# Both ends of a decoder kernel: operand tiles ahead of the squares, three products ahead of the norm's sums, the second weight load behind x, the last weight slot by token block

## The reference, cut to what matters

```python
def rmsnorm(x, g):
    xf = x.astype(jnp.float32)
    y = xf * lax.rsqrt(jnp.mean(xf * xf, axis=-1, keepdims=True) + EPS)
    return (y * g.astype(jnp.float32)).astype(x.dtype)
# first: the input norm and the projections of layer 0
hn = rmsnorm(h, mix_norm[i])
proj = hn @ w_in            # queries, keys, values, gates of two mixers
# last: the expert layer's sum and the final norm
a = (jax.nn.gelu(hid, approximate=False) * g).astype(xb.dtype)
return jnp.einsum('thk,thkd->td', a, ve)
...
return rmsnorm_2(h, final_norm_w)
```

## Time and profile before

| what | value |
| --- | --- |
| median of 3 runs | 3516.91 us (3513.79 to 3517.32) |
| the profiled execution | 3521.62 us |
| its span | 3519.7 us |
| mean granted TensorE clock | 0.993 |

### The profile page before, as it was taken

The page is one execution under the profiler, slowest core; times in us unless marked ns, Lnnn a source line. Parts: engine busy times, 40 slices in busy tenths (PEclk is TensorE's granted clock), DMA queues, the critical chain, the costliest instruction groups (busy, mean ns, idle before and its releaser), DMA issues. The chain is left out here.

```text
span 3519.7 us, 45047 instructions
## 1 busy us (share of the span) xinstructions
PE 3443.8 (98%) x16298; PEld 2801.3 (80%) x16298; DVE 1716.3 (49%) x3318; ACT 925.6 (26%) x1581; POOL 2181.6 (62%) x2180
## 2 busy tenths in 40 slices
PE   7998999999999999999999999999999999999998
PEld 5765888887688888877788777788888888888887
DVE  6563444247754424246324766655555154444443
ACT  3354222124622212135411111133333211111111
POOL 5421766675266667653367777655555588888885
PEclk9999999999999999999999999999999999999999
DMA  6110222222122222221122233344444665555552
GB/s 207 60 37 24 90 96 97 99 92 96 37 102 96 96 96 96 102 72 61 66 84 102 109 137 131 134 165 180 180 180 179 226 217 194 194 195 194 195 198 86
DMA packets 134325, 440.14 MB, mean 125 GB/s; under 512 B 7139, under 2 KB 76932, under 8 KB 97284
## 3 DMA queue, kind: packets, MB, share of 16 engines
q1 hardware_dynamic: 39168, 285.23, 22.9%
q10 hardware_dynamic: 94980, 152.40, 12.2%
HBM read 362.64 MB, written 74.96 MB: 124 GB/s over the span
## 5 line engine op out<-in xcount | busy, mean ns | idle before, releaser
L192 PE MATMUL banks<-memory,weights_split 128*128 128x512 f32 x9456 | 2248.1, 395 | 40.1 <-DMA memory<-in_consts 17.2
L192 PEld LDWEIGHTS banks<-memory,weights_split 128*128 128x128 f32 x9456 | 1760.4, 189 | 435.8 <-issue 51.0
L2984 POOL TENSOR_SCALAR weights_split<-weights_raw 128x512 fp32r<-128x512 f32 x1088 | 740.6, 690 | 1314.9 <-PE banks L192 669.3
L2989 POOL TENSOR_TENSOR weights_split<-weights_raw,weights_split 128x512 fp32r<-128x512 f32 x1088 | 1488.5, 1379 | 0.0
L192 PE MATMUL banks<-weights_split,memory 128*128 128x512 f32 (+1 forms) x3648 | 822.1, 387 | 1.9 <-DVE memory L1365 1.9
L192 PEld LDWEIGHTS banks<-weights_split,memory 128*128 128x128 f32 x3648 | 678.9, 188 | 141.5 <-DVE memory L1365 2.3
L2746 DVE TENSOR_TENSOR memory<-memory,memory 128x512 fp32r<-128x512 f32 x128 | 167.5, 1309 | 355.0 <-ACT memory L2860 355.0
L2725 DVE TENSOR_SCALAR memory<-banks,memory 128x128 f32<-128x128 f32 x512 | 174.3, 402 | 214.0 <-PE banks L2592 204.9
L2860 ACT ACTIVATE memory<-memory 128x512 fp32r<-128x512 f32 x128 | 80.8, 632 | 601.0 <-PE banks L192 587.9
L2793 ACT ACTIVATE memory<-banks 128x512 f32<-128x512 f32 x128 | 76.5, 597 | 569.2 <-PE banks L192 569.2
L2740 DVE TENSOR_TENSOR memory<-memory,memory 128x512 f32<-128x512 f32 x128 | 164.9, 1289 | 51.2 <-DMA memory<-hidden 44.7
(11 more groups left out here) (243 smaller groups left out, 2195.0 us busy)
## 6 DMA issues: line engine op xcount, KB each, us to landing
weights_raw<-in_weights SPq DMA_DIRECT2D x272, 1024.0 KB, 4.8
hidden<-memory ACTq DMA_DIRECT2D x64, 512.0 KB, 2.6
routing<-memory ACTq DMA_DIRECT2D x16, 2048.0 KB, 6.3
memory<-routing ACTq DMA_DIRECT2D x32, 1024.0 KB, 8.0
memory<-hidden ACTq DMA_DIRECT2D x32, 1024.0 KB, 10.2
window_rows<-memory ACTq DMA_DIRECT2D x1, 3064.0 KB, 25.3
chunk_rows<-memory ACTq DMA_DIRECT2D x1, 2556.0 KB, 12.8
residual<-in_x ACTq DMA_DIRECT2D x4, 512.0 KB, 11.2
```

The costliest lines, as they stand in the source:

```text
L192: last = k.nc.tensor.matmul(out, left[a], right[b], start=start and n == 0, stop=stop and n == 2, skip_group_check=True)
L2984: k.nc.gpsimd.tensor_scalar(cut(high, n * PIECE, PIECE), cut(raw, n * PIECE, PIECE), 1.0, 1.0, ALU.mult, ALU.mult).then_inc(k.high_made, 1)
L2989: k.nc.gpsimd.tensor_tensor(cut(low, n * PIECE, PIECE), cut(raw, n * PIECE, PIECE), cut(high, n * PIECE, PIECE).bitcast(F32), ALU.subtract ...
```

## The change

The first norm gets a stage of its own: ScalarE waits for the columns, does a one-element Square, makes the eight high parts, and then the eight squares, each in a buffer of its own; VectorE makes all low parts and then adds the squares. TensorE does three products, then waits for the constants, then does the sums, the bias rows and the other seven products. Its wait for the clearing of the scores and the scans moves into step 1 of the schedule, behind the first share. VectorE's part of the bias rows stands behind the evacuation of product 2. SP waits for the first part of x ahead of its load of slot 1. At the end, ScalarE does a one-element Sqrt after its last operand, and TensorE walks the last slot block by block with both keys in each bank.

```diff
-def first_norm(k, normed, await_input, await_consts):
+def first_norm(k, normed, await_columns, await_input, await_consts):
     normed.begin()
+    with k.scope(at=B_AT):
+        squares, spare = [k.take(512) for _ in range(D_TILES)], k.take(8)
...
     def scalar(act):
+        a = k.nc.scalar
+        await_columns(act)
+        a.activation(spare[:, 0:1], k.column(normed.gain, 0), ACT.Square)
         for n in range(D_TILES):
             await_input(act, n)
-            normed.scalar_tile(act, n)
+            a.activation(normed.out.high(n), tile(n), ACT.Copy, scale=k.column(normed.gain, n)).then_inc(k.x_high, 1)
+        for n in range(D_TILES):
+            a.activation(squares[n], tile(n), ACT.Square).then_inc(k.squared, 1)
         await_consts(act)
     def vector(dve):
         for n in range(D_TILES):
-            normed.vector_tile(dve, n)
+            dve.wait_ge(k.x_high, normed.out.made_before + n + 1)
+            v.scalar_tensor_tensor(out=normed.out.low(n), in0=tile(n), scalar=k.column(normed.gain, n),
+                                   in1=normed.out.high(n).bitcast(F32), op0=ALU.mult, op1=ALU.subtract).then_inc(k.x_low, 1)
+        for n in range(1, D_TILES):
+            dve.wait_ge(k.squared, normed.squared + n + 1)
+            if n > 1:
+                dve.wait_ge(k.summed, normed.summed + n - 1)
+            v.tensor_tensor(normed.total, squares[0] if n == 1 else normed.total, squares[n],
+                            ALU.add).then_inc(k.summed, 1)
         await_consts(dve)
-    def tensor(pe):
-        await_consts(pe)
...
-    made = [Bank(k, "vector")]
+    made = [Bank(k, "vector") for _ in range(3)]
     normed.reserve_sums()
-    made.append(Bank(k, "vector"))
     rows.reserve()
-    made += [Bank(k, "vector") for _ in range(8)]
+    made += [Bank(k, "vector") for _ in range(7)]
...
-        opening(0)
+        for n in range(3):
+            opening(n)
+        await_consts(pe)
         normed.tensor_sums(pe)
-        opening(1)
         rows.tensor(pe)
-        for n in range(2, 10):
+        for n in range(3, 10):
             opening(n)
-        pe.wait_ge(cleared, 6)
-        pe.wait_ge(scanned, 4 * HG_HEADS)
...
             advance(share)
+            if t == 1:
+                pe.wait_ge(cleared, 6)
+                pe.wait_ge(scanned, 4 * HG_HEADS)
...
-        rows.vector(dve)
         for n in range(2, 10):
             evacuate(made[n], out, SB_DIM ** -0.5 if n == 8 else 1.0)
+            if n == 2:
+                rows.vector(dve)
...
+            else:
+                pe.wait_ge(ready, e + 2)
+                for b in range(BLOCKS):
+                    for half in range(2):
+                        begun, _ = apply(e, b, half)
+                        if b == 0 and half == 0:
+                            k.release_previous(begun, slot % RING)
+                        _, last = apply(e + 1, b, half)
                         last.then_inc(out_filled, 1)
...
+        a.activation(spare[:, 0:1], k.const("eps"), ACT.Sqrt)
         for b in range(BLOCKS):
...
             for place in range(RING):
+                if place == 1:
+                    sp.wait_ge(k.inputs_in[0], 16)
                 load(place, place, None)
```

More of the change, by code:

```diff
@@ L523, in load_embedding, with tile @@
     return Stage(scalar=scalar, meet=False)
-def first_norm(k, normed, await_input, await_consts):
+def first_norm(k, normed, await_columns, await_input, await_consts):
     normed.begin()
+    with k.scope(at=B_AT):
+        squares, spare = [k.take(512) for _ in range(D_TILES)], k.take(8)
+    def tile(n):
+        return cut(k.h, n * 512, 512)
     def scalar(act):
+        a = k.nc.scalar
+        await_columns(act)
+        a.activation(spare[:, 0:1], k.column(normed.gain, 0), ACT.Square)
         for n in range(D_TILES):
             await_input(act, n)
-            normed.scalar_tile(act, n)
+            a.activation(normed.out.high(n), tile(n), ACT.Copy, scale=k.column(normed.gain, n)).then_inc(k.x_high, 1)
+        for n in range(D_TILES):
+            a.activation(squares[n], tile(n), ACT.Square).then_inc(k.squared, 1)
         await_consts(act)
     def vector(dve):
+        v = k.nc.vector
         for n in range(D_TILES):
-            normed.vector_tile(dve, n)
+            dve.wait_ge(k.x_high, normed.out.made_before + n + 1)
[7 more added lines that the diff above has]
+                            ALU.add).then_inc(k.summed, 1)
         await_consts(dve)
-    def tensor(pe):
-        await_consts(pe)
-    return Stage(tensor, vector, scalar, meet=False)
+    return Stage(None, vector, scalar, meet=False)
 def normed_heads(k, normed, tiles, evacuate, parts, width, value_of, meet=False):
@@ L897, in opening_layer @@
     normed = Norm(k, "mix0", hn, common, by_token=True)
-    load, await_input, await_consts = load_inputs(k)
-    normed_first = first_norm(k, normed, await_input, await_consts)
+    load, await_columns, await_input, await_consts = load_inputs(k)
+    normed_first = first_norm(k, normed, await_columns, await_input, await_consts)
     rows = BiasRows(k)
@@ L2503, in expert_layer @@
         kept.append(k.take(GROUP * TOKENS))
-        result_sums, deviation, rstd = k.take(2 * BLOCKS), k.take(2 * BLOCKS), k.take(BLOCKS)
+        result_sums, deviation, rstd, spare = k.take(2 * BLOCKS), k.take(2 * BLOCKS), k.take(BLOCKS), k.take(8)
     with k.scope(at=B_AT):
@@ L2621, in tensor, with apply @@
                        skip_group_check=True)
-        for e in range(PEER_KEYS):
+        def apply(e, b, half):
+            place = (value_first + e // 2) % RING
+            values = [k.ring[:, (2 * place + side) * SLOT + e % 2 * D_MODEL:
+                             (2 * place + side) * SLOT + (e % 2 + 1) * D_MODEL] for side in range(2)]
+            return split_product(
+                k, out_banks[2 * b + half].memory, [x[:, b * P:(b + 1) * P] for x in operand(e % 4)],
+                [w[:, half * 512:(half + 1) * 512] for w in values], False, e == PEER_KEYS - 1)
@@ L2623, in tensor @@
+        for e in range(0, PEER_KEYS, 2):
             slot = value_first + e // 2
[L2624 to L2627, removed]
+            k.slot_begins(pe, slot % RING, slot // RING)
             pe.wait_ge(ready, e + 1)
[L2629 to L2636, removed]
+            if e < PEER_KEYS - 2:
+                for b in range(BLOCKS):
+                    for half in range(2):
+                        begun, last = apply(e, b, half)
+                        if b == 0 and half == 0:
+                            k.release_previous(begun, slot % RING)
+                last.then_inc(used, 1)
+                pe.wait_ge(ready, e + 2)
+                for b in range(BLOCKS):
+                    for half in range(2):
+                        _, last = apply(e + 1, b, half)
+                last.then_inc(used, 1)
+            else:
+                pe.wait_ge(ready, e + 2)
+                for b in range(BLOCKS):
+                    for half in range(2):
+                        begun, _ = apply(e, b, half)
+                        if b == 0 and half == 0:
+                            k.release_previous(begun, slot % RING)
+                        _, last = apply(e + 1, b, half)
@@ L2637, in tensor @@
                         last.then_inc(out_filled, 1)
-            if e < PEER_KEYS - 1:
-                last.then_inc(used, 1)
     def vector(dve):
@@ L2900, in load, with await_columns @@
         act.dma_start(k.consts[:, :], k.dram["consts"]).then_inc(consts_in, 16)
+    def await_columns(act):
+        act.wait_ge(columns_in, 16)
     def await_tile(act, n):
-        if n == 0:
-            act.wait_ge(columns_in, 16)
         if n % 2 == 0:
@@ L2909, in await_consts @@
         eng.wait_ge(consts_in, 16)
-    return load, await_tile, await_consts
+    k.inputs_in = x_in
+    return load, await_columns, await_tile, await_consts
 def program(nc, dram):
```

## The result

The changed kernel takes 3500.2 us in the median of 5 runs (3496.3 to 3500.6), the one before 3516.9 (3513.8 to 3518.8). The ratio is 0.995 with a 95% interval of 0.9938 to 0.9962, so 13 to 22 us are gone. The forecast was 3496.4, 20.5 us less; the measured 16.7 lie inside the range, and the interval does not tell them apart.

The account below looks back on a forecast made before the run. TensorE, busy 98% of the span, was taken as the bound, so only its idle, lower-clock and tail time could fall. 17.4 us at the start plus 3.1 at the end, off 3516.9, gave 3496.4 us; range 3491 to 3503.

Parts of the forecast that it names:

- The steps at the start: Timeline up to the first cross product, forecast at 77.6 us where it was 94.97: 17.4 us earlier.
- the total: VectorE's seven additions of the first norm's squares, forecast to end at 27.6 us, 2.5 us before TensorE's sums need them.
- One step: Opening transfers: slot 1 shares with x's tiles 4 to 7 from about 10.5 us, both landing at 15.4.
- A term: VectorE's eight low parts in the first norm: 1.09 us each, back to back except a wait for tile 6, ending at 18.4.
- Rival (a): First norm: VectorE and GpSimd alternate, a low part costs 2.03 us, 7.1 us are lost, giving 3503.5 us; 7%.
- The sum: Whole kernel: 17.4 us at the start plus 3.1 at the end, 20.5 us less in all.
- The tail: After the last matmul: finishing block by block with the table preloaded saves 3.1 us (2.9 to 3.5).
- (b): Start: x comes no earlier (up to 2.6 us) or the clock falls in product 0 (3.4 us): 3499 to 3500 us; 22%.
- (c): Cross products: VectorE's chain sets their pace, so the start's gain is given back: 3514 us with the tail alone; 3%.
- (d): Opening products: late sums leave bank 0 not free, TensorE stops at product 5, slower at 3518 us; 1%.

Follow-up runs that it names:

- experiment 3: The changed kernel without SP's wait, so the load of slot 1 is issued at once; median 3501.4 us, first cross product at 81.56 us.
- 5: The changed kernel with GpSimd pausing in the first slot, after two pieces and the third's high part, until the eighth low part; median 3497.2 us.
- 8: The changed kernel with only the eight gain columns loaded ahead of x, the rest behind it, and the last block sent in halves; median 3496.6 us.
- 12: The changed kernel with GpSimd pausing in the first slot until the sixth low part and the last block sent in halves; median 3496.5 us.
- Before again: The kernel before, unchanged, run and profiled again; median 3516.6 us, ratio 0.9993 to the kernel before.
- 2: The kernel before with only the new order of the last slot and the spare root; median 3516.2 us, ratio 0.9992.
- 11: The kernel before with only TensorE's wait for the constants moved behind product 0; 3513.5 us in one run.
- experiment 6: The changed kernel with the norm's sums behind product 0 instead of behind product 2; median 3509.9 us, ratio 0.9984 to the kernel before.
- 7: The changed kernel with the wait for the cleared scores back ahead of the value products; median 3503.1 us.
- 9: The changed kernel without the one-element root at the end; 3502.1 us in one run, 6.18 us from last matmul to end.
- experiment 10: The changed kernel with the last two keys one after the other, keeping the one-element root; 3498.2 us in one run, tail 8.44 us.

## Why the prediction was right

**The steps at the start held almost to the tenth, in part by luck.** Product 0's last low part was forecast for 18.4 and came at 18.41; the total for 27.6, came at 27.57; the sums for 30.1, at 30.21; the first evacuation for 39.9, at 40.19; the scores were clear at 72.97 (73.2), and the first cross product came at 77.12 (77.6). The start gave 17.85 us against 17.4, half a microsecond of it because the issue gap behind the bias rows did not show. Two of these marks are luck. The total I had made of four additions at 1.78 and three at 0.68, with GpSimd done with slot 1 at 25.8; the seven ran from 0.91 to 1.60 each, with GpSimd busy there until 28.7. And the five other profiles with the same norm and transfers end the low parts at 18.4 to 19.1 and the total at 27.5 to 29.0. Nothing hung on the total: in the changed kernel's order the sums waited for it in none of them.

**One step was wrong and cost nothing.** I had slot 1 and the last tiles of x share the transfers and land together at 15.4. The last part of x landed at most 9.3 us after its issue, which was at about 2.9, so at about 12; slot 1 let GpSimd start only at 17.70. x went first, and the constants too (issued at 3.35, landed 13.3 us later, at 16.7), which I had left out of what slot 1 shares with. Since no engine waited for a later part of x, its earlier landing brought nothing, and product 2, which reads slot 1, found its first half split in time.

**A term was missing in form and nearly right in size.** I took 1.09 us for every low part and one short wait for x; there was no wait, but the eight took 1.16 in the mean. The eight came to 9.27 us (up to 9.83 in the other profiles with that code) against the 9.05 forecast, since both errors are small and of opposite sign. Experiments 3, 5, 8 and 12 show them at 10.98, 6.78, 10.95 and 7.22 with more or less of GpSimd beside them, so 0.85 to 1.37 us each. Rival (a) had the direction (the more GpSimd, the slower) and not the size: 2.03 in the mean was never seen, and the longest single one took 1.83. The Trainium skill (SBUF — State Buffer, "SBUF: two separate sides") has the one of the two that starts second blocked for the whole instruction of the first; that is more than these runs show. While the eight low parts of experiment 3 ran, 10.98 us, GpSimd did eight whole instructions: four high and four low parts of weights, 0.62 and 1.26 us each alone. One after another the sixteen would take, by estimate, 8 x 0.74 + 4 x 0.62 + 4 x 1.26 = 13.4 us, so they overlapped in part.

**The sum was too large for the medians, by 3.8 us,** which the interval covers; part of it can be traced. I counted 5.0 us of lower clock in the start of before as if every execution had it, in the sums (1.5), product 1 (1.6) and the value matmuls (1.9). Before again has it once more; experiments 2 and 11 have pauses as long and only 1.1 to 1.7 us of that cost: their starts are 91.58 and 91.22. The four profiles of the old start have a mean of 93.1, the four of the new one 77.5, so a typical gain of the start is nearer 15.6 us than 17.85; with 3.3 of the tail that is 18.9. The first profile of before had drawn the dear case, and the medians see the mean. The middle does not explain the two profiles' surplus, since it is 3415.3 and 3415.2 in them, but it varies from 3410.6 to 3417.8 us, with no relation to the edits that these runs show, and medians of five move with it. The last 2 us, from 18.9 to 16.7, stay open within that. What the change takes away, part by part: 8.1 us of pause for the total (and the clock behind it, 12.7 together, experiment 6), 3.8 to 4.4 by the order of the transfers (3), 1.9 to 2.2 at the clearing (7), 3.3 in the tail (9, 10). These overlap and do not add up.

**The tail:** 3.3 us against 3.1. The last square ended 0.64 us behind TensorE's last matmul where I took 0.71, and from there to the scalings 0.84 us passed where I took 0.95. I had named the load of the table as a cause of the old lateness; it is 1.0 us of it in the old order (experiment 10) and none in the new one (9).

**The rivals.** (b): x came earlier, and the clock fell in product 0 in none of the ten profiles with the new start. That it can happen experiment 11 shows, where it fell there in the old norm's trickle, beside waits of 1.11 and 1.73 us; my reason against it, that a fall needs a pause of 1.9 us or more, was too strong. The longest wait in the new product 0 was 0.74 us. (c): no wait in the cross products grew, three of 4.6 us in all before and after, and the middle is equal in the two first profiles. (d): product 5 found its bank free: the seven products behind the bias rows run without a gap.

Open: what decides whether a pause of 1.86 us brings the lower clock (8.02 us for 27 matmuls) or not (6.42 in experiments 2 and 11, 6.46 in 7). No run here chose it, only drew it.

## What to carry to other kernels

The wait that heads an engine's list may be worth nothing: the constants' 17.2 us hid a chain on VectorE that ended later in any case. What moved the start most was other products put into that chain's shadow. By the timelines they can stand there because the low parts now come ahead of the squares (product 0 needs the eighth, made at 29.2 before and at 18.4 now); no run takes the one without the other. When the last stage drains bank by bank, finish the output block by block, so that the drain of all but one block lies under TensorE; here it was worth 2.3 us or more, preloading the table 1.0 at most. And before a difference of two profiles is taken for the gain, see by a second profile of the same kernel which low-clock stretches are always there and which are drawn.

## What the runs showed of the hardware that was not expected

- The same program has 4.6 us more or less in one stretch of 300 us, at equal busy time, by the granted clock (0.98, 0.99, 1.00), though one core runs alone. (4.6 is the difference of the middles of before and before again, and 20 matmuls in the window from 2000 to 2300 us make as much.)
- A load of 1 MB issued just ahead of x delayed x's landing by about 2.7 us (median 8.4 to 11.0 us from issue). Held back behind x's first part, it did not slow the rest of x visibly: from the first part's landing to the last one's it is about 3.8 us in both, 8.4 to 12.2 and 11.1 to 14.9.
- VectorE's two-input instruction at 128x512 took 0.74 us at the least and 1.75 at the most beside GpSimd's splitting. Eight of them took from 6.78 to 10.98 us, by how much GpSimd worked beside them, and GpSimd's own instructions grew with them, from 0.62 to 1.05 us and from 1.26 to 1.71.
- TensorE's granted clock fell behind a pause of 1.86 us at the clearing in two of five profiles with that pause, at the same place of the program.
